# Strassen's identity in half the contraction of a second attention projection, and running product sums kept in one PSUM bank

## The chip, the core and the metric

The kernel runs on one core of one Trainium2 chip. The metric is the device time of one execution in microseconds (us). Three runs of the kernel before gave 2095.98 us in the median, 2095.78 at the least and 2096.19 at the most. PE is TensorE, DVE is VectorE, ACT is ScalarE, POOL is GpSimd and SP is SyncE.

## What is computed

The reference is a stack of layers on a sequence of 256 tokens with 2048 features, all in fp32. A Mamba-2 mixer, a sliding-window attention with a gate, a neighbourhood attention and a squared-ReLU MLP with 8192 hidden features follow each other, each with a residual. The part that the change touches most is the end of the neighbourhood attention and what comes next:

```python
def second_block(x, ...):
    hn = rms_norm(x, norm_mix[layer])
    x = x + neighbourhood_attention(hn, na_w_qkv, ..., na_w_o)   # ends with out @ w_o, 2048 x 2048
    x = x + sq_relu_mlp(rms_norm(x, norm_mlp[layer]), mlp_w1[layer], mlp_w2[layer])
```

`out @ w_o` is a product of 256 x 2048 with 2048 x 2048. The sliding-window attention ends in a product of the same size (`o @ w_out`), and the second half of the MLP (`(a * a) @ w2`) is 256 x 8192 with 8192 x 2048.

## The kernel before, in words

**Units.** All the matrix products are cut into units, 381 of them, listed by `plan` (line 114). A unit is one tile of weights of 128 x 2048 fp32 numbers, 1 MB, that comes from HBM by one DMA (`load`, L997, on SP's queue). Each fp32 number is split into two parts that TensorE multiplies in its fp32r type: ACT copies the tile to `whi` (`high`, L1461), which rounds it, and DVE writes the rest, `wlo = raw - whi` (`low`, L1893). The activations are kept split in the same way, in A1h and A1l or A2h and A2l. A product is then the sum of three: high by high, low by high, high by low.

A unit of form B ("token block") is 512 columns of the result and four 128-row steps of the contraction, for two tiles of 128 tokens: 2 x 4 x 3 = 24 matmuls of 128 x 512 (L1168, L1170, L1172). A unit of form A ("feature block") is 128 columns of the result over the whole contraction. A unit of form P is one product of Strassen's identity in Winograd's form (`product_block`, L1184, L1186, L1188): one token tile only, so 12 matmuls. Seven P units, named a to g in the order a, c, b, d, e, f, g, take the place of four B units: two 512-column blocks ("left" and "right") by two groups of four contraction steps. The other contraction steps of these two blocks stay B units, two for each block.

**What a set of seven needs.** Products b, c, d and f multiply sums of activations. `mixed` (L1921 on DVE, L1838 on ACT, L1924 on DVE) makes them: four additions or subtractions of 128 x 512, four high parts, four low parts. Products b, d, f and g multiply sums of weights. For b and f the second weight tile is added by a DMA from POOL's queue that accumulates into the buffer (`acc`, L2645), and for d and g DVE adds two buffers (`add`, L1904). The results go to the blocks of the residual XR by `drain`: product a is copied by ACT out of its bank to SBUF (`kept`, L1476), d and f are added to that copy by DVE (L1932), and the running sum a, a+d, a+d+f is added to XR (L1860, L1955) from there. A set has 11 such DVE operations and the copy. Eight sets exist: one in the output projection of the sliding-window attention (stage `bo`, products `bp`), and seven in the MLP's second product (stage `down`, products `dp`), where DVE's factor is a column of SM.

**Order of the work.** One list, `script` (line 240), is read by every engine, and each engine takes from it what is its own, in that order, with semaphore waits between. At the step of unit u stand, in this order: the late work on unit u-1 (drain of its last bank), the high split of unit u+2 (it waits until TensorE has done unit u-1, since whi and wlo have three buffers), the low split of unit u+2, sums of weights, the matmuls of u with the drain of its first token tile between, the load of unit u+5, and then what `timetable` (line 174) puts behind unit u. What is put there is written out by hand: attention steps, the activation sums ("mix"), and "x3".

**The stages around the change.** The neighbourhood attention's last group of four heads, step ("na", 3, 0 to 8), ends inside the units of stage `no`: steps 4 to 8 run at units no,0,0 to no,0,2. Stage `no` is sixteen B units: blocks 0 to 3, four contraction groups each. Their results are added to XR (L2086). After block c is complete, the two steps ("x3", c, 0) and ("x3", c, 1) run, one and two units later. The first turns the block with eight transposes on TensorE (`turned`, L1296) and scales, splits and stores it in A1: per chunk, ACT does one scaled copy and one high part twice over (L1688, L1696), DVE two scaled copies and two low parts (L2330, L2339), and each low and high part waits for what the other engine made. The second takes the squares for the RMS norm on ACT (L1706). Chunk c is needed by unit upb,c, the first units of the MLP. The step ("x3", c, 0) stands at unit no,c+1,0 for c = 0, 1, 2, and at upb,0 for c = 3.

Raw tiles go to a ring of three SBUF buffers, of four in some stretches (`wide_ring`, line 454), and the summed weights of a set of seven to one more ("chain", in the work area W). Four PSUM banks serve the units before the MLP in turn. The four others, the side banks, serve attention steps, transposes and the products a, b, d, f of `bp`. In the MLP a planner deals out all eight: each new block takes the bank that has been free longest.

Of the kernel before, what the change touches and what calls it, by code (L numbers as in the profile page):

```python
# [7 lines left out]
P = 128  # L8
# [85 lines left out]
def pair_of(tag):  # L94

    return (1, 2) if tag[0] == "bp" else (2 * tag[2], 2 * tag[2] + 1)


def products(tag):


    top, low = (8, 12) if tag[0] == "bp" else (16 * tag[1] + 8, 16 * tag[1] + 12)
# [11 lines left out]
def plan():  # L114
# [31 lines left out]
    u += in_turn("-a-c-b-d-e-fg--", sevens("bp", "b_w_out", -1, 0),  # L146
# [4 lines left out]
    for nb in range(ND):  # L151
        u += b(("no", nb), "na_w_o_2", nb * 512)
# [21 lines left out]
def timetable(units):  # L174
# [38 lines left out]
    after[at["bo", 2, 0]].append(("mix", -1))  # L213
# [14 lines left out]
    for c in range(ND):  # L228
        run(("x3", c), at["no", c, 3] + 1, 4 if c == ND - 1 else 2)
# [88 lines left out]
def shut(tag):  # L318

    if tag[0] == "down" and seven(tag[1], tag[2]):  # L320
        return (1,) if tag[2] % 2 and tag[3] == 1 else ()
    if tag[0] == "bo" and tag[1] in (1, 2):
        return (1,) if tag[1:] == (2, 1) else ()
    return (0, 1) if tag[0] == "ao" or tag[-1] == 3 else ()


def drains(tag):

    left, right = pair_of(tag)
    return {"a": (), "b": ((1, right, 1), (0, right, 1)), "c": ((0, right, 1),),
            "d": ((0, left, 1), None, (0, right, -1)), "e": ((0, left, 1),), "f": (None, (1, right, -1), (1, left, 1)),
            "g": ((1, left, 1),)}[tag[3]]


def block_of(u, tag, t):
# [5 lines left out]
    return {"c": (s, right, 0), "e": (s, left, 0), "g": (s, left, 1)}.get(name, (u,))  # L343
# [48 lines left out]
def stack_kernel(nc, wst, first, xtok, pos, cols, rows, nabias, consts, out):  # L392
# [7 lines left out]
    with ExitStack() as ctx:  # L400
# [53 lines left out]
        def wide_ring(u):  # L454

            return at["bo", 2, 1] <= u <= at["bo", 3, 3] or u >= at["up", 0, 9]
# [20 lines left out]
        def raw_of(u):  # L477
            if RAW[u] < MLP_ONLY:
                return raw[:, RAW[u], :]
            c = M_RING if RAW[u] == MLP_ONLY else M_CHAIN + 2048 * (RAW[u] - RING)  # L480
# [48 lines left out]
        bp = {x: at["bp", -1, 0, x] for x in "abcdefg"}  # L529
        CLOSES = {(2, 0): (bp["c"], 0), (2, 1): (at["bo", 2, 1], 1), (1, 0): (bp["e"], 0), (1, 1): (bp["g"], 0)}  # L530
        for u, (form, tag, *_) in enumerate(units[:at["up", 0, 4]]):
            if form == "A":
                blocks = [0]
            elif form == "P":
                if tag[3] in "ceg":
                    _, nb, t = block_of(u, tag, 0)
                    BANK[u, 0] = BANK[at["bo", nb, 0], t]
# [7 lines left out]
            for t in blocks:  # L545
                owner = ((u, t) if form == "A" or tag[0] == "ao" else
                         CLOSES.get((tag[1], t), (at.get(tag[:-1] + (3,)), t)) if tag[0] == "bo" else
# [82 lines left out]
        def att_act():  # L630
# [34 lines left out]
        mix_v = Marks(sem("mix_v"), *[words("1 3 2 4 l1 l3 l2 l4")] * (QT + 1))  # L665
        mix_a = Marks(sem("mix_a"), *[words("h1 h3 h2 h4")] * (QT + 1))
# [5 lines left out]
        SIDE, side_before, side_next = {}, [None] * 4, 0  # L672
        EMPTIES = {
# [11 lines left out]
            "bp": lambda x: keep_a(bp["a"]) if x == "a" else evac_v((bp[x], {"b": 1, "d": 1, "f": 0}[x])),  # L685
        }

        def side_uses(s):
# [51 lines left out]
            elif what == "mm" and units[r[0]][1][0] == "bp" and units[r[0]][1][3] in "abdf":  # L740
                yield ("bp", units[r[0]][1][3]), None
# [8 lines left out]
        for x in "abdf":  # L750
            BANK[bp[x], 0] = 4 + SIDE["bp", x][0]
            BEFORE[bp[x], 0] = None, SIDE["bp", x][1]

        def side_free(use):
# [3 lines left out]
        keep_a = Marks(sem("product_kept"), [s[1] for s in SCRIPT if s[0] == "late" and units[s[1]][0] == "P" and  # L758
                                             units[s[1]][1][3] == "a"])


        DRAINS, PIECE, PIECES, EMPTIED = {}, {}, {}, {}
        for s in SCRIPT:
            u = s[1] if len(s) > 1 else None
            if s[0] in ("evac", "late") and units[u][1][0] in ("bo", "bp"):
# [7 lines left out]
        for key, piece in DRAINS.items():  # L773
            u, n = key
            if piece:
                PIECE[key], PIECES[piece[:2]] = PIECES.get(piece[:2]), key
            if not piece or units[u][0] == "B" or None not in drains(units[u][1]):
                EMPTIED[block_of(u, units[u][1], n if units[u][0] == "B" else 0)] = key
        for x in "abcdefg":
            DRAINS.update({(bp[x], n): piece for n, piece in enumerate(drains(units[bp[x]][1]))})  # L780
        FIRST = ((bp["c"], 0), (bp["d"], 0), (bp["f"], 2))
        LAST = {(bp["d"], 2): (0, 2), (bp["e"], 0): (0, 1), (bp["f"], 1): (1, 2), (bp["g"], 0): (1, 1)}
# [4 lines left out]
        for u, (form, tag, *_) in enumerate(units):  # L787
            if u < at["up", 0, 4]:
                continue
            for t in range(NT if form == "B" else 1):  # L790
                block = block_of(u, tag, t) if form != "A" else (u,)
                if block not in WHERE:
                    i = min(range(8), key=lambda i: pool[i][0])
                    WHERE[block], BEFORE[u, t] = i, pool[i][1:]
                    copied = form == "P" and tag[3] == "a"
                    key = u if copied else (u, 0) if form == "A" else EMPTIED[block]
                    assert pool[i][0] <= u, (u, pool)
                    pool[i] = [u + 1 if copied else key[0] + 1, keep_a if copied else evac_v, key]
# [30 lines left out]
        def mix_of(s):  # L829

            c = W_GS if s < 0 else M_MIX
            return W[:, c:c + 2048]

        def parts_of(s):
# [5 lines left out]
            else:  # L840
                yield "1", A1h[:, 0:4, 0:P], A1l[:, 0:4, 0:P], a[:, 1, :, 1, :]
# [7 lines left out]

        def kept(u):  # L850
            if units[u][1][0] == "bp":
                return W[:, W_KT:W_KT + 512]
            c = M_HB + units[u][1][2] * 512
            return W[:, c:c + 512]
# [90 lines left out]
        def residual_ready(t, c, stage):  # L945
# [9 lines left out]
            if stage == "ln1":  # L955
                ends = {(2, 0): (bp["d"], 2), (2, 1): (bp["f"], 1), (1, 0): (bp["e"], 0), (1, 1): (bp["g"], 0)}
                return evac_v(ends[c, t] if c in (1, 2) else (at["bo", c, 3], t))
            if stage == "no":
                return aff_v(("a", t, c), 1)
            return evac_v((at["no", c, 3], t))  # L960
# [1819 lines left out]
```

## Time and profile before

| | |
|---|---|
| median of the three runs | 2095.98 us |
| the profiled execution, its own time | 2096.38 us |
| its span in the profile | 2094.6 us |
| outside the span (launch and end) | 1.8 us |
| TensorE busy in the span | 2088.4 us, 10850 matmuls |
| VectorE busy | 1560.2 us (74%) |
| ScalarE busy | 1144.0 us (55%) |
| DMA | 411.82 MB, 197 GB/s in the mean |

The page gives for every group of instructions the busy time and the mean time of one in ns. A matmul's record overlaps the next one's, so what it costs is the distance between starts and not its own length. In a timeline each row is the start in us from the start of the span, the length in us, the engine, the line of the kernel, and in brackets the idle time of the engine before it with what ended it. `x3` behind a row means three instructions merged.

### The profile page before, as it was taken

The numbers are of one execution on the slowest core, as the hardware profiler recorded it, in microseconds if no ns is written. First come the engines' busy times: TensorE is split into PE (matmuls) and PEld (weight loads), VectorE is DVE, ScalarE is ACT, GpSimd is POOL, SyncE is SP. The second block draws the span as 40 slices with busy tenths as digits, with TensorE's granted clock in tenths as the row PEclk, the third lists the DMA queues.
The fourth block names the chain that finished last, engine by engine and source line by source line (L and its number), as shares of the span: only waits on it lengthen the run. The fifth ranks groups of instructions, "written<-read, shape, count | busy, mean of one in ns | idle before, by whom it ended". The sixth has DMA issues, their size and how long they took to land.

```text
span 2094.6 us, 27475 instructions
## 1 busy us (share of the span) xinstructions
PE 2088.4 (100%) x10850; PEld 1765.6 (84%) x10850; DVE 1560.2 (74%) x2067; ACT 1144.0 (55%) x1425; POOL 53.6 (3%) x44
## 2 busy tenths in 40 slices
PE   9999999999999999999999999999999999999999
PEld 8888888888887888888788888888888888888887
DVE  7798787777778867768875566556778688688775
ACT  6777565565564555665555445454545445444452
POOL 0000000000000000000010011000000000000000
PEclk9999999999999999999999999999999999999999
DMA  8565555564554744447564554455576666566663
GB/s 324 194 239 191 195 210 191 200 211 178 205 192 150 247 160 146 157 151 231 191 211 171 189 181 171 164 181 203 200 221 212 209 221 199 219 188 198 241 181 141
DMA packets 67425, 411.82 MB, mean 197 GB/s; under 512 B 7392, under 2 KB 14304, under 8 KB 19808
## 3 DMA queue, kind: packets, MB, share of 16 engines
q1 hardware_dynamic: 64992, 393.28, 52.3%
q0 software_dynamic: 2304, 16.78, 4.4%
q8 instruction: 86, 1.41, 0.3%
q14 instruction: 43, 0.35, 0.0%
HBM read 407.80 MB, written 2.23 MB: 196 GB/s over the span
## 4 chain that ended last, share of the span: by engine, by line
PE 99%; DVE 1%; ACT 0%; issue 0%; POOL 0%
PE bank L1146 27%; PE bank L1168 15%; PE bank L1170 15%; PE bank L1172 15%; PE bank L1151 14%; PE bank L1188 2%; PE bank L1184 2%; PE bank L1186 2%; PE bank L1266 1%; PE bank L1401 1%; PE bank L1337 1%; PE bank L1359 0%; PE bank L1389 0%; PE bank L1268 0%; PE bank L1296 0%; PE bank L1245 0%
## 5 line engine op out<-in xcount | busy, mean ns | idle before, releaser
L1893 DVE TENSOR_TENSOR wlo<-raw,whi 128x2048 fp32r<-128x2048 f32 x314 | 718.5, 2289 | 217.6 <-ACT whi L1461 186.9
L1461 ACT ACTIVATE whi<-raw 128x2048 fp32r<-128x2048 f32 x314 | 600.2, 1912 | 250.9 <-PE bank L1172 230.7
L1146 PE MATMUL bank<-A,whi 128*128 128x512 f32 x2448 | 587.7, 392 | 0.0
L1146 PEld LDWEIGHTS bank<-A,whi 128*128 128x128 f32 x2448 | 451.1, 188 | 91.8 <-issue 2.4
L1151 PEld LDWEIGHTS bank<-A,wlo 128*128 128x128 f32 x2432 | 311.8, 191 | 11.8
L1151 PE MATMUL bank<-A,wlo 128*128 128x256 f32 x2432 | 315.3, 283 | 0.0
L1168 PE MATMUL bank<-whi,A2h 128*128 128x512 f32 x768 | 301.2, 392 | 0.0
L1170 PE MATMUL bank<-whi,A2l 128*128 128x512 f32 x768 | 299.3, 390 | 0.0
L1172 PE MATMUL bank<-wlo,A2h 128*128 128x512 f32 x768 | 299.1, 389 | 0.0
L1168 PE MATMUL bank<-whi,A 128*128 128x512 f32 x608 | 241.7, 398 | 0.0
L1170 PE MATMUL bank<-whi,A 128*128 128x512 f32 x608 | 237.2, 390 | 0.1
L1172 PE MATMUL bank<-wlo,A 128*128 128x512 f32 x608 | 237.3, 390 | 0.0
L1893 DVE TENSOR_TENSOR wlo<-W,whi 128x2048 fp32r<-128x2048 f32 x63 | 144.2, 2291 | 52.8 <-ACT whi L1461 52.1
L1168 PEld LDWEIGHTS bank<-whi,A2h 128*128 128x128 f32 x768 | 144.2, 188 | 31.0 <-issue 1.4
L1172 PEld LDWEIGHTS bank<-wlo,A2h 128*128 128x128 f32 x768 | 144.2, 188 | 30.4
L1170 PEld LDWEIGHTS bank<-whi,A2l 128*128 128x128 f32 x768 | 144.2, 188 | 29.5
L1461 ACT ACTIVATE whi<-W 128x2048 fp32r<-128x2048 f32 x63 | 120.2, 1914 | 86.5 <-DVE W L1904 55.4
L1168 PEld LDWEIGHTS bank<-whi,A 128*128 128x128 f32 x608 | 114.3, 188 | 24.6 <-issue 2.1
L1172 PEld LDWEIGHTS bank<-wlo,A 128*128 128x128 f32 x608 | 114.1, 188 | 24.6 <-DVE wlo L1873 0.6
L1170 PEld LDWEIGHTS bank<-whi,A 128*128 128x128 f32 x608 | 114.4, 188 | 24.1 <-DVE A L2319 1.0
L1498 ACT ACTIVATE W<-bank 128x256 f32<-128x256 f32 x60 | 23.1, 384 | 179.8 <-PE bank L1151 179.8
L1860 DVE SCALAR_TENSOR_TENSOR XR<-bank,SM,XR 128x512 f32<-128x512 f32 x110 | 80.7, 746 | 18.7 <-PE bank L1172 16.8
(267 smaller groups left out, 1897.6 us busy)
## 6 DMA issues: line engine op xcount, KB each, us to landing
raw<-wst SPq DMA_DIRECT2D x308, 1024.0 KB, 4.8
W<-wst SPq DMA_DIRECT2D x37, 1024.0 KB, 4.9
W<-wst POOLq DMA_DIRECT2D x10, 1024.0 KB, 8.3
W<-cum_scratch SPq DMA_DIRECT2D x8, 1024.0 KB, 7.0
raw<-wst POOLq DMA_DIRECT2D x6, 1024.0 KB, 8.0
W<-rows SPq DMA_DIRECT2D x21, 256.0 KB, 5.9
W<-first SPq DMA_DIRECT2D x12, 384.0 KB, 7.6
W<-exp_scratch SPq DMA_DIRECT2D x16, 256.0 KB, 6.4
```

The lines of the kernel that those rows point to most:

```text
L1146: last = e.matmul(o[:, :], whi[:, s, k * P:(k + 1) * P], A1[:, k, :, :].rearrange("p h t -> p (h t)"), start=k == 0, stop=packed and k == ...
L1151: last = e.matmul(o[:, T:2 * T], wlo[:, s, k * P:(k + 1) * P], A1h[:, k, :], start=False, stop=k == KT - 1)
L1168: e.matmul(o, h, wh, start=opens and k == 0, stop=False)
L1170: e.matmul(o, low, wh, start=False, stop=False)
L1172: last = e.matmul(o, h, wl, start=False, stop=t in shut(tag) and k == 3)
L1184: e.matmul(o, h, wh, start=name in ("a", "b", "d", "f") and k == 0, stop=False)
L1186: e.matmul(o, low, wh, start=False, stop=False)
L1188: last = e.matmul(o, h, wl, start=False, stop=k == 3)
L1461: e.activation(whi[:, u % 3, :], raw_of(u), ACT.Copy).then_inc(*hi.inc((u, 3)))
L1498: e.activation(W[:, M_R + i % 4 * T:M_R + (i % 4 + 1) * T], rest, ACT.Copy).then_inc(*rest_a.inc(u))
L1860: return e.scalar_tensor_tensor(out=o, in0=a, scalar=s, in1=b, op0=op0, op1=op1)
L1893: e.tensor_tensor(wlo[:, u % 3, :], raw_of(u), whi[:, u % 3, :], ALU.subtract).then_inc(*lo.inc((u, 3)))
```

## The change

The neighbourhood attention's output projection gets a set of seven: in blocks 1 and 2, for contraction steps 8 to 15, the four B units become seven P units of a new kind `np` (left is block 2, right is block 1). Stage `no` becomes no,0,0 to no,0,3, then no,1,0; a; no,1,1; c; no,2,0; b; no,2,1; d; no,3,0; e; no,3,1; f; g; no,3,2; no,3,3. Its mix has an addition more, since the heads' outputs are only there as high and low part: DVE first adds A2h and A2l in two operations of 128 x 1024. The mix stands behind no,1,0, before ("x3", 0, 0), which stays there. Steps ("x3", 1, ...) and ("x3", 2, ...) move back to no,3,2, no,3,3 and upb,0. Second, in all the sets the running sum stays in one PSUM bank: d and f accumulate onto a, DVE drains the bank after each of the three, and the copy on ACT and DVE's two additions to it are gone. The core of the diff:

```diff
     u += b(("bo", 0), "b_w_out", 0)
-    u += in_turn("-a-c-b-d-e-fg--", sevens("bp", "b_w_out", -1, 0),
+    u += in_turn("-a-c-b-d-e-fg--", sevens("bp", "b_w_out", -2, 0),
...
-    for nb in range(ND):
-        u += b(("no", nb), "na_w_o_2", nb * 512)
+    u += b(("no", 0), "na_w_o_2", 0)
+    u += in_turn("-a-c-b-d-e-fg--", sevens("np", "na_w_o_2", -1, 0),
+                 [("B", ("no", nb, i), "na_w_o_2", 4 * i, nb * 512) for nb in (1, 2, 3) for i in range(4 if nb == 3 else 2)])
...
-    after[at["bo", 2, 0]].append(("mix", -1))
+    after[at["bo", 2, 0]].append(("mix", -2))
+    after[at["no", 1, 0]].append(("mix", -1))
...
-    for c in range(ND):
-        run(("x3", c), at["no", c, 3] + 1, 4 if c == ND - 1 else 2)
+    run(("x3", 0), at["no", 0, 3] + 1, 2)
+    after[at["no", 3, 2]].append(("x3", 1, 0))
+    after[at["no", 3, 3]] += [("x3", 1, 1), ("x3", 2, 0)]
+    after[at["upb", 0]].append(("x3", 2, 1))
+    run(("x3", 3), at["no", 3, 3] + 1, 4)
...
-    return {"a": (), "b": ((1, right, 1), (0, right, 1)), "c": ((0, right, 1),),
-            "d": ((0, left, 1), None, (0, right, -1)), "e": ((0, left, 1),), "f": (None, (1, right, -1), (1, left, 1)),
-            "g": ((1, left, 1),)}[tag[3]]
+    return {"a": ((0, left, 1),), "b": ((1, right, 1), (0, right, 1)), "c": ((0, right, 1),), "d": ((0, right, -1),),
+            "e": ((0, left, 1),), "f": ((1, right, -1), (1, left, 1)), "g": ((1, left, 1),)}[tag[3]]
...
         def wide_ring(u):
-            return at["bo", 2, 1] <= u <= at["bo", 3, 3] or u >= at["up", 0, 9]
+            return (at["bo", 2, 1] <= u <= at["bo", 3, 3] or at["no", 1, 1] <= u <= at["no", 3, 3] or
+                    u >= at["up", 0, 9])
...
+        for kind, p in (("bp", bp), ("np", np_)):
+            for x in "ab":
+                BANK[p[x], 0] = 4 + SIDE[kind, x][0]
+                BEFORE[p[x], 0] = None, SIDE[kind, x][1]
+            for x, before in (("d", "a"), ("f", "d")):
+                BANK[p[x], 0] = BANK[p["a"], 0]
+                BEFORE[p[x], 0] = evac_v, (p[before], 0)
...
             def load(u):
...
+                    elif RAW[u] >= MLP_ONLY and stage_of(u) == 1 and (before is None or not stage_of(before)):
+                        w.wait_ge(*na_p("v3", 3))
...
             def product_block(u, o):
-                    e.matmul(o, h, wh, start=name in ("a", "b", "d", "f") and k == 0, stop=False)
+                    e.matmul(o, h, wh, start=name in ("a", "b") and k == 0, stop=False,
+                             skip_group_check=name in ("d", "f"))
...
             def late(u):
-                if form == "P" and tag[3] == "a":
-                    w.wait_ge(*mm_done(u))
...
-                    e.activation(kept(u), bank[BANK[u, 0]][:, :], ACT.Copy).then_inc(*keep_a.inc(u))
...
             def mixed(s):
+                elif s == -1:
+                    w.wait_ge(*na_a("h3", 3))
+                    w.wait_ge(*na_v("l3", 3))
+                    for q in range(2):
+                        k = slice(8 + 4 * q, 12 + 4 * q)
+                        e.tensor_tensor(mix_of(s)[:, q * 1024:(q + 1) * 1024].rearrange("p (k t) -> p k t", k=4),
+                                        A2h[:, k, :], A2l[:, k, :], ALU.add).then_inc(*mix_v.inc(f"x{q}", s + 2))
+                    w.wait_ge(*mix_v("x1", s + 2))
...
             def drain(u, n):
-                if not DRAINS[u, n]:
-                    w.wait_ge(*(evac_v((u, 0)) if tag[3] == "d" else evac_v((product(u, "d"), 2))))
-                    e.tensor_tensor(kept(u), ps, kept(u), ALU.add).then_inc(*evac_v.inc((u, n)))
-                    return
```

In the work area, the raw buffer of the fourth ring place in stage `no` is W from N_KT on, and the chain buffer lies over NS and PT. Both are read by the attention's last step until its value products are done (`na_p("v3", 3)`), and so SP waits for these before the load of a.

## Rows read from the trace of the kernel before

**Rows 1.** The page, parts 1, 2 and 4.

```profile
PE 2088.4 (100%) x10850; PEld 1765.6 (84%) x10850; DVE 1560.2 (74%) x2067; ACT 1144.0 (55%) x1425; POOL 53.6 (3%) x44
...
PEclk9999999999999999999999999999999999999999
...
PE 99%; DVE 1%; ACT 0%; issue 0%; POOL 0%
```

**Rows 2.** Stretches: busy us of PE, PEld, DVE, ACT, POOL; clock; DMA share; GB/s.

```profile
949.84:952.56 2.72, 2.72 (x13) 2.25 (x12) 2.62 (x5) 2.08 (x4) 0.00 (x0) 1.00 1.04 220
958.00:960.80 2.80, 2.80 (x14) 2.26 (x12) 2.61 (x3) 1.92 (x1) 0.00 (x0) 1.00 0.21 23
1340.89:1362.75 21.86, 21.86 (x99) 18.06 (x98) 12.57 (x10) 10.99 (x12) 0.00 (x0) 1.00 0.50 190
1492.98:1555.89 62.91, 62.91 (x278) 51.83 (x277) 52.77 (x40) 31.91 (x22) 1.76 (x3) 1.00 0.67 212
```

**Rows 3.** Timeline of TensorE: last attention products, transposes of chunk 0, a wait in bo.

```profile
1324.73 1.89 PE L1401 MATMUL bank<-W 128*128 128x256 f32 x8
...
1340.10 1.03 PE L1296 MATMUL bank<-KO,XR 128*128 128x128 f32 x8
...
1008.26 0.63 PE L1278 MATMUL bank<-KO,XR 128*128 128x128 f32 x4 [0.59 <-DVE XR L2283]
```

**Rows 4.** Timeline of VectorE, stage bo, from unit bo,2,0 to product c.

```profile
946.68 2.29 DVE L1893 TENSOR_TENSOR wlo<-W,whi 128x2048 fp32r<-128x2048 f32 x1 [0.92 <-ACT whi L1461]
...
949.49 2.86 DVE L1921 TENSOR_TENSOR W<-W 128x512 f32<-128x512 f32 x4
952.26 0.69 DVE L1924 TENSOR_TENSOR A<-W,A 128x512 fp32r<-128x512 f32 x1
952.87 1.89 DVE L1924 TENSOR_TENSOR mixr<-W,mixr 128x512 fp32r<-128x512 f32 x3
954.92 4.58 DVE L1893 TENSOR_TENSOR wlo<-raw,whi 128x2048 fp32r<-128x2048 f32 x2 [0.16 <-issue]
```

**Rows 5.** Timeline of ScalarE in the same stretch.

```profile
950.20 0.63 ACT L1838 ACTIVATE A<-W 128x512 fp32r<-128x512 f32 x1 [3.62 <-DVE W L1921]
950.93 2.09 ACT L1838 ACTIVATE mixr<-W 128x512 fp32r<-128x512 f32 x3
952.92 1.91 ACT L1461 ACTIVATE whi<-raw 128x2048 fp32r<-128x2048 f32 x1
```

**Rows 6.** Timeline of VectorE, stage no, from unit no,1,0 on.

```profile
1336.93 2.29 DVE L1893 TENSOR_TENSOR wlo<-raw,whi 128x2048 fp32r<-128x2048 f32 x1 [1.39 <-ACT whi L1461]
1340.74 0.88 DVE L2330 TENSOR_SCALAR W<-bank,CO 128x256 f32<-128x256 f32 x2 [1.51 <-PE bank L1296]
1342.47 0.69 DVE L2339 TENSOR_TENSOR A<-W,A 128x512 fp32r<-128x512 f32 x1 [0.86 <-ACT A L1696]
1343.56 0.69 DVE L2339 TENSOR_TENSOR A<-W,A 128x512 fp32r<-128x512 f32 x1 [0.40 <-ACT A L1696]
```

**Rows 7.** Timeline of ScalarE in the same stretch.

```profile
1334.91 1.92 ACT L1461 ACTIVATE whi<-raw 128x2048 fp32r<-128x2048 f32 x1 [3.52 <-PE bank L1172]
1341.17 0.48 ACT L1688 ACTIVATE W<-bank,CO 128x256 f32<-128x256 f32 x1 [4.34 <-PE bank L1296]
1341.74 0.63 ACT L1696 ACTIVATE A<-W 128x512 fp32r<-128x512 f32 x1
...
1343.36 1.90 ACT L1461 ACTIVATE whi<-raw 128x2048 fp32r<-128x2048 f32 x1
1345.17 0.61 ACT L1706 ACTIVATE W<-XR 128x512 f32<-128x512 f32 x1
...
1346.69 1.92 ACT L1461 ACTIVATE whi<-raw 128x2048 fp32r<-128x2048 f32 x1
```

**Rows 8.** Stage bo: SP issues product a and the tile behind it; the first lands.

```profile
934.70 0.81 SPq L997 DMA_DIRECT2D W<-wst  x2
...
939.55 1.92 ACT L1461 ACTIVATE whi<-W 128x2048 fp32r<-128x2048 f32 x1 [3.38 <-DMA W<-wst]
```

More of the change, by code:

```diff
@@ L342, in block_of @@
     left, right = pair_of(tag)
-    return {"c": (s, right, 0), "e": (s, left, 0), "g": (s, left, 1)}.get(name, (u,))
+    return {"c": (s, right, 0), "e": (s, left, 0), "g": (s, left, 1), "b": (u,)}.get(name, ("sum", s, p))
 def pieces12(x, n):
@@ L739, in side_uses @@
                 yield ("upb", r[0]), r[0]
-            elif what == "mm" and units[r[0]][1][0] == "bp" and units[r[0]][1][3] in "abdf":
-                yield ("bp", units[r[0]][1][3]), None
+            elif what == "mm" and units[r[0]][1][0] in ("bp", "np") and units[r[0]][1][3] in "ab":
+                kind, *_, name = units[r[0]][1]
+                yield (kind, name), None if kind == "bp" else 2 + (name in "bf")
         for s in SCRIPT:
@@ L764, in stack_kernel @@
             u = s[1] if len(s) > 1 else None
-            if s[0] in ("evac", "late") and units[u][1][0] in ("bo", "bp"):
+            if s[0] in ("evac", "late") and units[u][1][0] in ("bo", "bp", "np"):
                 continue
@@ L774, in stack_kernel @@
             u, n = key
[L775 to L782, printed above, removed]
+            PIECE[key], PIECES[piece[:2]] = PIECES.get(piece[:2]), key
+            EMPTIED[block_of(u, units[u][1], n if units[u][0] == "B" else 0)] = key
+        for p in (bp, np_):
+            for x in "abcdefg":
+                DRAINS.update({(p[x], n): piece for n, piece in enumerate(drains(units[p[x]][1]))})
+        LAST = ((bp["d"], 0), (bp["e"], 0), (bp["f"], 0), (bp["g"], 0))
         pool = [[holds[i][0] + 1, evac_v if units[holds[i][0]][1][0] not in ON_ACT else evac_a, holds[i]]
@@ L794, in stack_kernel @@
                     WHERE[block], BEFORE[u, t] = i, pool[i][1:]
[L795 to L796 removed]
+                    key = (u, 0) if form == "A" else EMPTIED[block]
                     assert pool[i][0] <= u, (u, pool)
[L798 removed]
+                    pool[i] = [key[0] + 1, evac_v, key]
+                elif form == "P" and tag[3] in "df":
+                    BEFORE[u, t] = evac_v, (product(u, "a" if tag[3] == "d" else "d"), 0)
                 BANK[u, t] = WHERE[block]
@@ L848, in stack_kernel @@
         xu = W[:, W_XU:W_XU + T]
[L850 to L854, printed above, removed]
         def hidden(i):
@@ L1084, in store @@
             def store(u, n):
-                if DRAINS.get((u, n)) and units[u][1][0] != "bp":
+                if DRAINS.get((u, n)) and units[u][1][0] not in ("bp", "np"):
                     t, nb, _ = DRAINS[u, n]
@@ L1205, in factor @@
                 which = {"b": "1", "c": "4", "d": "2", "f": "3"}[name]
-                return h, low, (mix_a("h" + which, s + 1), mix_v("l" + which, s + 1))
+                return h, low, (mix_a("h" + which, s + 2), mix_v("l" + which, s + 2))
             def dt(n):
@@ L1836, in mixed @@
                 for name, high, _, x in parts_of(s):
-                    w.wait_ge(*mix_v(name, s + 1))
-                    e.activation(high, x, ACT.Copy).then_inc(*mix_a.inc("h" + name, s + 1))
+                    w.wait_ge(*mix_v(name, s + 2))
+                    e.activation(high, x, ACT.Copy).then_inc(*mix_a.inc("h" + name, s + 2))
             def upb(t, n):
```

93 lines of the change are left out of this document (47 added, 46 removed).

## The prediction

> **What bounds the kernel now.** The page comes first: TensorE is busy in all but 6 us of the 2094.6 us span, it is 99% of the chain that ended last, and its clock stands at the upper level in every slice [rows 1]. So only two things can move the time: what TensorE has to do, and how long it stands without work. The stretches come next, since they give what a unit costs. Four B units in a row (96 matmuls) take 21.86 us, 5.46 each. A P unit on A2 takes 2.72 us, one that reads the mixed sums 2.80. In stage `down`, through a whole set of seven, TensorE is busy 62.91 of 62.91 us while DVE is busy 52.77 [rows 2]. DVE is therefore the engine with the least room beside TensorE wherever P units run. The timelines of DVE and ACT in stages `bo` and `no` then show how near the splits are to being late. They are what decides here.
>
> **TensorE's work.** Removed are four B units of stage `no`: 21.86 us. Added are seven P units: a, b, e, g at 2.72, c, d, f at 2.80, in all 10.88 + 8.40 = 19.28 us [rows 2]. The eight transposes of a chunk, 0.79 us between the starts of the first and of the next unit (1340.10 to 1340.89 [rows 2, 3]), are as many as before. Saved: 2.58 us, or 0.12%. With every cover kept that is the whole gain.
>
> **The running sums in one bank.** Per set DVE does 9 drains instead of 11 operations, at about 0.69 us each (as all its 128 x 512 work [rows 4]), and ACT one copy less. That frees about 1.4 us of DVE per set, seven times in the MLP. I cost it at nothing, because TensorE does not wait in the set of seven that the stretch shows [rows 2]; the work that ends last there is TensorE's own. The new waits (d until a is drained, f until d is) are three to four units long, 8 us and more against a drain of 0.69. The sum's bank is held from a to f, but of eight banks I count at most six in use at that point. In `bo` the new drain of a stands between the low splits of c and of bo,1,0: it moves the second from 957.2-959.5 to 957.9-960.1, and bo,1,0 starts at 960.80 (c ends there [rows 2, 4]). Hidden.
>
> **What the mix and x3 do to product c.** This term decides. In `bo`, DVE starts the mix at 949.49, its four operations take 2.86, ACT's four high parts end in time for the high split of c at 952.92, and DVE's low parts end in time for its low split at 954.92, done at 957.2. TensorE starts c at 958.00 [rows 2, 4, 5]. The spare time is 0.8 us, and 1.3 up to the third matmul, the first to need wlo.
>
> In `no` I put the same on the clock of the trace. Unit no,1,0 runs 1334.64 to 1340.10, the transposes to 1340.89 [rows 3], a to 1343.61, no,1,1 to 1349.07, and there c wants whi, and at 1349.5 wlo.
> - DVE is free for the mix at 1336.93 + 2.29 = 1339.2, after the low split of no,1,1 [rows 6].
> - New: two additions of 128 x 1024. The trace has 0.69 us for 512 columns and 2.29 for 2048 [rows 4], so about 1.2 each (bounds 0.69 and 2.29; in between by their columns): 1341.6.
> - Four mixes as in `bo`, 2.86: 1344.5. ACT's high parts end 952.92 - 949.49 = 3.4 us after the mixes' start: 1345.0. DVE's low parts end 5.3 after it: 1346.9 [rows 4, 5].
> - Then, before the high split of c in the common order, comes ("x3", 0, 0). DVE's scaled copies can start only at 1346.9 instead of 1340.74. ACT's first copy is done by then; its first high part starts when DVE's first copy is done, 0.5 later, at 1347.4. From that high part to the next high split it is 1343.36 - 1341.74 = 1.6 us: 1349.0 [rows 6, 7].
> - High split of c, 1.9: 1350.9. Low split, 2.29: 1353.2.
>
> So c's first matmul waits 1.9 us, and its third until 1353.2 instead of 1349.5: TensorE loses 3.7 us. It ends c at 1355.5. Behind the high split, ACT has the squares of chunk 0 (1345.17 to 1346.69, 1.5 us [rows 7]) and then the high split of no,2,0: 1352.4 to 1354.3; its low split ends 1356.7, wanted at 1356.0: 0.7 more. In all 4.4 us. Who waits: only TensorE; DVE's and ACT's later work is paced by it.
>
> After that DVE catches up: going on in the same way, the low splits of b, no,2,1 and d come 1.2 us or more before they are wanted, the addition of weights for d (128 x 2048, so about 2.29) included. The rest that a set adds (three high and three low splits more, two weight additions, nine drains for four) runs in `down` beside TensorE without a wait and leaves DVE 10 of 62.91 us [rows 2]; I cost it at nothing. Without that cover each low split would cost its 2.29.
>
> **The loads.** SP stops at the load of a until the attention's last value products are done, about 1326.6 [rows 3], with the loads of no,1,1, c and no,2,0 queued behind. In `bo` two tiles were issued together from 934.70 and the first was there at 939.55 [rows 8], 4.85 us. So a is there at about 1331.5, its splits (1.92 and 2.29) end at 1335.7, the two additions of block 0 to XR (0.69 each) at 1337.1, and the low split of no,1,1 starts 0.2 later than its 1336.93 before [rows 6]. I take 0 to 0.2, inside the rounding of the term above. POOL's accumulating load for b is issued when a is split, 25 us before b starts.
>
> **The end of the stage.** Three chunks of x3 now run in consecutive units. One needs on ACT 2.2 us (1341.17 to 1343.36), squares 1.5, a high split 1.9, together 5.6 against 6.25 us of TensorE (5.46 + 0.79) [rows 3, 7]. On DVE it is about 4.6 with its waits and a low split 2.29, 6.9, which slips by 0.6 per unit, against some 5 us of lead. The transposes of chunk 3 want the last drain of no,3,3 some 0.2 us after it is done. I take 0, bounds 0 and 1.
>
> **Sum.** -2.58 + 3.7 + 0.7 + 0 = +1.8 us. The profiled execution took 2096.38 us, which gives 2098.2; it stands 0.4 above the median of 2095.98, which gives 2097.8. A measurement of this kernel can tell about 0.2%, 4.2 us, from no change: faster means under 2091.8, slower over 2100.2. The lost time lies between 0 (the chain comes in time) and about 6 (handoffs between ACT and DVE as wide as the 0.40 and 0.86 us seen before low parts [rows 6], the additions at their upper bound).
>
> **Rivals.**
> 1. *The cover holds.* ACT gets c's high split in before 1347, as in `bo`. For it speaks that the same pattern ran in `bo` without a wait; against it that there no x3 step and no additions stood before c. Only the gain is left: 2096.0 - 2.6 = 2093.4.
> 2. *The clock falls at c* (the slower side). TensorE's longest wait in stages `bo` and `no` is 0.59 us [rows 3] and no slice is under the upper level of 2.4 GHz [rows 1], so the trace says nothing of what a stand of 3.7 us, broken by two matmuls, does. If the clock fell to 1.2 GHz behind it, the matmuls of c, no,2,0 and b (11 us) or a part of them would take twice as long: 2 to 8 us more, 2100 to 2106, with 2103 in the middle. It decides only if c starves as forecast. The Trainium skill has such a rule ("TensorE: Matmul & The Clock Gate", Why this matters for your kernels): a long enough gap between bursts of matmuls sends the clock back to half. By that rule the sum would be this rival's; no row here has such a gap.
> 3. *The loads come together* (slower too). If the four queued tiles shared the bandwidth evenly (4.2 MB at the 220 GB/s of rows 2: 19 us), a would land at 1345.6 and not at 1331.5. Up to 1.5 us of lateness hides; the mix would start some 13 us late, and TensorE would lose that: about 2111. Against it stand the 4.85 us of the first of two [rows 8].
> 4. *The sums in one bank are worth time after all*, in a stretch of the MLP where TensorE waits unseen: up to 5 us faster, 2091. TensorE's 6 us outside its busy time over the whole span [rows 1] speak against it. If, the other way, d or f waited for a drain, each of the seven sets would show it.
>
> **Chances.** Starved at c, clock kept: 0.67, alone 2095.2 to 2100.0. Rival 1: 0.19. Rival 2: 0.08. Rival 3: 0.04. Rival 4: 0.02. Faster by over 0.2% comes from rival 4 alone: 0.02. Slower by over 0.2% from rivals 2 and 3 and the upper edge of the first case: 0.15. Within 0.2%: 0.83. The range for 8 in 10 takes in rival 1 and the first case: 2093.2 to 2100.2.
>
> **What the changed profile would show.** 10838 matmuls, bar lost records. In stage `no` a wait of TensorE for whi at c's first matmul of about 1.9 us, then one for wlo of about 1.8, then 0.7 in no,2,0, and none after. On DVE the two 128 x 1024 additions of about 1.2 us directly before four mixes, and x3's copies behind the last low part. On ACT the high split of c behind x3's second high part. Stage `down` at the same 62.9 us. The forecast is wrong if c starts without a wait, if TensorE waits at a or at upb, or if the granted clock leaves the upper level in that stage.

## The result, and the profile after

The changed kernel takes 2099.39 us (median of 22 runs, 2097.25 to 2101.22), the kernel before 2096.16 in as many (2095.57 to 2097.97): a ratio of 1.0014, 95% interval 1.0008 to 1.002. That is 3.2 us more, 1.6 above the forecast, inside its range and within 0.2%. The profiled execution took 2099.29 us, 2.9 more than that of before.

The page of the changed kernel, parts 1 and 4, beside [rows 1]:

```profile
PE 2087.7 (100%) x10838; PEld 1764.6 (84%) x10838; DVE 1567.9 (75%) x2072; ACT 1148.2 (55%) x1424; POOL 55.4 (3%) x46
...
PE 95%; DVE 2%; ACT 1%; DMA 1%; SPq 0%; issue 0%; POOL 0%; DVEq 0%; ACTq 0%
```

TensorE has 12 matmuls less and is busy only 0.7 us less, where 2.6 were to go; and TensorE's share of the chain that ended last has fallen from 99 to 95%. The waits of TensorE there, 1320 to 1420 us (line and what it waited for: us in total, times, longest):

```profile
PE bank L1202 <- DVE wlo L1900: 1.7, 1, 1.7
PE bank L1197 <- ACT whi L1475: 1.5, 1, 1.5
```

Both belong to product c. TensorE's timeline around it:

```profile
1348.96 0.39 PE L1185 MATMUL bank<-wlo,A2h 128*128 128x512 f32 x1
1350.86 0.50 PE L1197 MATMUL bank<-whi,mixr 128*128 128x512 f32 x1 [1.51 <-ACT whi L1475]
1351.19 0.39 PE L1200 MATMUL bank<-whi,mixr 128*128 128x512 f32 x1
1353.24 0.50 PE L1202 MATMUL bank<-wlo,mixr 128*128 128x512 f32 x1 [1.66 <-DVE wlo L1900]
...
1354.33 0.63 PE L1197 MATMUL bank<-whi,mixr 128*128 128x512 f32 x1
1354.76 0.63 PE L1200 MATMUL bank<-whi,mixr 128*128 128x512 f32 x1
...
1357.32 0.54 PE L1183 MATMUL bank<-whi,A2l 128*128 128x512 f32 x1
1357.69 0.39 PE L1185 MATMUL bank<-wlo,A2h 128*128 128x512 f32 x1
```

The two waits stand where they were forecast, and the third matmul starts at 1353.24 for 1353.2. The third wait of the forecast, 0.7 us in no,2,0, is not there. New is what follows from 1354.33 on: the matmuls start 0.43 us apart instead of 0.23. The stretch of its own (columns as in [rows 2]) says why:

```profile
1354.20:1357.60 3.40, 3.40 (x10) 2.65 (x9) 3.40 (x3) 2.04 (x2) 0.00 (x0) 0.50 0.21 27
```

The granted clock is at half, 1.2 GHz, for 3.4 us; just before it and behind it the clock is at 2.4 (1.00 from 1354.00 to 1354.10, 0.94 from 1357.60 to 1357.70). The stretch is too short to show in the page's 40 slices. Here the Trainium skill ("TensorE: Matmul & The Clock Gate", Why this matters for your kernels) has the rule that a long enough gap between bursts of matmuls sends the clock back to half; the trace agrees in direction, since the clock fell behind two gaps, of 1.5 and 1.7 us, with two matmuls between them.

DVE and ACT, beside [rows 6, 7]:

```profile
1339.19 2.35 DVE L1922 TENSOR_TENSOR W<-A2h,A2l 128x1024 f32<-128x1024 f32 x2
1341.58 2.87 DVE L1936 TENSOR_TENSOR W<-W 128x512 f32<-128x512 f32 x4
...
1344.97 1.89 DVE L1939 TENSOR_TENSOR mixr<-W,mixr 128x512 fp32r<-128x512 f32 x3
1346.77 0.87 DVE L2342 TENSOR_SCALAR W<-bank,CO 128x256 f32<-128x256 f32 x2
...
1350.89 2.29 DVE L1900 TENSOR_TENSOR wlo<-raw,whi 128x2048 fp32r<-128x2048 f32 x1 [1.09 <-ACT whi L1475]
```

```profile
1331.55 1.92 ACT L1475 ACTIVATE whi<-W 128x2048 fp32r<-128x2048 f32 x1 [4.46 <-DMA W<-wst]
...
1345.02 0.46 ACT L1695 ACTIVATE W<-bank,CO 128x256 f32<-128x256 f32 x1
1347.28 0.63 ACT L1703 ACTIVATE A<-W 128x512 fp32r<-128x512 f32 x1 [1.80 <-DVE W L2342]
...
1348.91 1.90 ACT L1475 ACTIVATE whi<-raw 128x2048 fp32r<-128x2048 f32 x1
```

The additions start at 1339.19 (forecast 1339.2), the mixes at 1341.58 (1341.6), DVE's low parts end at 1346.8 (1346.9), c's high split starts at 1348.91 (1349.0) and its low split at 1350.89 (1350.9). Before it, ACT stands 1.80 us for DVE's scaled copy of x3: that is the late step that holds c up. The load of a is there at 1331.55 (1331.5).

To compare kernels without what varies elsewhere, I measure stage `no` from the last value products of the attention to the transposes of chunk 3: 1324.73 to 1408.07 before, 83.34 us; 1324.78 to 1410.94 after, 86.16. These 2.8 us are the whole difference between the two profiled executions, within 0.1 us. TensorE's timeline of the changed kernel at these two places:

```profile
1324.78 1.89 PE L1415 MATMUL bank<-W 128*128 128x256 f32 x8
...
1410.94 1.03 PE L1310 MATMUL bank<-KO,XR 128*128 128x128 f32 x8
```

### The profile page after: what moved, and what is told of

Same layout as the page of the kernel before. It is cut to its first block, busy times and chain, and to the rows that moved or that the text cites. A ratio compares the mean times of both kernels' runs of the same rounds, so it can differ in the third digit from the quotient of the medians.

```text
span 2097.5 us, 27442 instructions
## 1 busy us (share of the span) xinstructions
PE 2087.7 (100%) x10838; PEld 1764.6 (84%) x10838; DVE 1567.9 (75%) x2072; ACT 1148.2 (55%) x1424; POOL 55.4 (3%) x46
## 4 chain that ended last, share of the span: by engine, by line
PE 95%; DVE 2%; ACT 1%; DMA 1%; SPq 0%; issue 0%; POOL 0%; DVEq 0%; ACTq 0%
PE bank L1159 26%; PE bank L1181 14%; PE bank L1183 14%; PE bank L1185 14%; PE bank L1164 13%; PE bank L1202 3%; PE bank L1197 3%; PE bank L1200 3%; DVE wlo L1900 1%; PE bank L1280 1%; PE bank L1415 1%; DMA raw<-wst 1%; PE bank L1351 1%; PE bank L1373 0%; PE bank L1403 0%
## 5 line engine op out<-in xcount | busy, mean ns | idle before, releaser
L1900 DVE TENSOR_TENSOR wlo<-raw,whi 128x2048 fp32r<-128x2048 f32 x310 | 709.2, 2288 | 206.5 <-ACT whi L1475 175.8
L1475 ACT ACTIVATE whi<-raw 128x2048 fp32r<-128x2048 f32 x310 | 592.2, 1912 | 229.9 <-PE bank L1185 207.0
L1181 PE MATMUL bank<-whi,A2h 128*128 128x512 f32 x736 | 288.8, 392 | 0.0
L1183 PE MATMUL bank<-whi,A2l 128*128 128x512 f32 x736 | 287.0, 390 | 0.0
L1185 PE MATMUL bank<-wlo,A2h 128*128 128x512 f32 x736 | 286.6, 389 | 0.0
L1900 DVE TENSOR_TENSOR wlo<-W,whi 128x2048 fp32r<-128x2048 f32 x70 | 160.1, 2290 | 62.9 <-ACT whi L1475 62.7
L1475 ACT ACTIVATE whi<-W 128x2048 fp32r<-128x2048 f32 x70 | 133.4, 1914 | 105.7 <-DVE W L1911 66.5
L1181 PEld LDWEIGHTS bank<-whi,A2h 128*128 128x128 f32 x736 | 138.4, 188 | 29.9 <-issue 1.4
L1185 PEld LDWEIGHTS bank<-wlo,A2h 128*128 128x128 f32 x736 | 138.3, 188 | 29.1
L1867 DVE SCALAR_TENSOR_TENSOR XR<-bank,SM,XR 128x512 f32<-128x512 f32 x138 | 100.9, 745 | 18.9 <-PE bank L1185 16.8
```

The source lines that it names most:

```text
L1181: e.matmul(o, h, wh, start=opens and k == 0, stop=False)
L1183: e.matmul(o, low, wh, start=False, stop=False)
L1185: last = e.matmul(o, h, wl, start=False, stop=t in shut(tag) and k == 3)
L1475: e.activation(whi[:, u % 3, :], raw_of(u), ACT.Copy).then_inc(*hi.inc((u, 3)))
L1867: return e.scalar_tensor_tensor(out=o, in0=a, scalar=s, in1=b, op0=op0, op1=op1)
L1900: e.tensor_tensor(wlo[:, u % 3, :], raw_of(u), whi[:, u % 3, :], ALU.subtract).then_inc(*lo.inc((u, 3)))
```

## Experiments

The theory (T): DVE comes too late for c since it has two additions and four mixes to do behind the low split of no,1,1; TensorE stands, and since it stands its clock falls. The rivals are these. R1: the drop of the clock is free or was there anyway, and the stand alone is the loss. R2: the running sums in one bank cost time as well. R3: the additional splits of the set cost time in the stage wherever its pre-work is put. The last column of this table splits the stage at c's third matmul, the first that needs wlo.

| kernel | median us (range, n) | ratio to before, 95% | mean clock | stage, us | to c's 3rd + from it |
|---|---|---|---|---|---|
| changed | 2099.39 (2097.25 to 2101.22, 22) | 1.0014, 1.0008 to 1.002 | 1.0 in 4, 0.999 in 13, 0.998 in 5 | 86.16 | 28.46 + 57.70 |
| changed, again | 2100.01 (2098.06 to 2100.97, 11) | 1.0016, 1.0007 to 1.0025 | 1.0 in 1, 0.999 in 6, 0.998 in 4 | 86.10 | 28.46 + 57.64 |
| x3 later | 2095.09 (2094.22 to 2095.82, 11) | 0.9992, 0.9983 to 1.0001 | 1.0 | 81.95 | other order |
| sums only | 2096.10 (2095.74 to 2097.79, 11) | 0.9998, 0.9989 to 1.0006 | 1.0 | 83.34 | no product c |
| fill | 2097.69 (2097.29 to 2099.24, 11) | 1.0006, 0.9997 to 1.0015 | 1.0 | 85.30 | 28.64 + 56.66 |
| mix early | 2093.54 (2092.68 to 2094.99, 11) | 0.9985, 0.9976 to 0.9994 | 1.0 | 80.94 | 24.88 + 56.06 |
| mix early, again | 2093.73 (2093.48 to 2094.92, 11) | 0.9987, 0.9978 to 0.9996 | 1.0 | 80.94 | 24.88 + 56.06 |
| additions twice | 2101.84 (2100.49 to 2103.19, 11) | 1.0026, 1.0017 to 1.0035 | 0.998 in all | 88.77 | 30.85 + 57.92 |
| twice and fill | 2100.62 (2099.85 to 2101.92, 11) | 1.0021, 1.0012 to 1.003 | 1.0 | 87.53 | 30.91 + 56.62 |
| x3 first | 2101.35 (2100.56 to 2102.55, 8) | 1.0025, 1.0015 to 1.0035 | 0.998 in all | 88.51 | 29.60 + 58.91 |

The kernel before took 2096.67 us beside the first four experiments (33 runs), 2096.27 beside the next four (29) and 2096.39 beside the last (15), which ran on another chip. Its stage `no` is 83.34 us long. In x3 later the transposes of chunk 0 stand behind c, so its two parts can't be set beside the others'. The length of the stage comes from one profiled execution of each kernel.

**x3 later.** The two steps of x3 for chunk 0 stand behind product d and the unit after it, and no longer behind no,1,0 and a:

```diff
-    run(("x3", 0), at["no", 0, 3] + 1, 2)
+    run(("x3", 0), at["np", -1, 0, "d"], 2)
```

> The steps of x3 for chunk 0 stand behind product d and unit no,3,0 instead of behind no,1,0 and a. Theory (c starves because x3's copies and high parts stand, in ACT's order, between the mix and the high split of c): ACT splits c from about 1345.1, DVE from 1346.9 to 1349.1; c starts 0.8 us earlier without the transposes before it, at 1348.3, and waits for wlo 0.3 to 0.5 us. The granted clock stays at its upper level. Span 2094.6 - 2.6 + 0.4 = 2092.4, time 2093.8 (2093.4 to 2094.5), ratio 0.9989. Rival A (the two additions and the mix starve c by themselves): a wait of 2 us or more stays at c, time 2096 or more. Rival B (the time was lost in the sets of the MLP, by waits for the one bank): no wait at c either way, time stays near 2099.

Measured 2095.09, and one wait left:

```profile
1349.66 0.50 PE L1202 MATMUL bank<-wlo,mixr 128*128 128x512 f32 x1 [0.43 <-DVE wlo L1900]
```

ACT no longer stands before the high split of c, so its first matmul does not wait. The low split is still late, since its engine had the additions and mixes to do: 0.6 us lost against the usual distance of 0.23. The stage is 1.4 us shorter than before and 4.2 shorter than with the change as made. So most of the loss, the clock's part included, hangs on x3's place between the mix and c's high split, and a part of the gain comes forth when it goes. The median is 0.6 us above the upper end of what was expected, and its interval still touches 1; the 1.6 us to the median of before agree with the stage's 1.4.

**Sums only.** Stage `no` as before, with four B units per block; of the change only the running sums in one bank stay:

```diff
-    u += b(("no", 0), "na_w_o_2", 0)
-    u += in_turn("-a-c-b-d-e-fg--", sevens("np", "na_w_o_2", -1, 0),
-                 ...
+    for nb in range(ND):
+        u += b(("no", nb), "na_w_o_2", nb * 512)
```

> The second half of the change alone: stage no has its sixteen plain units as before, the running sums stay in one PSUM bank in the eight other sets. Theory (no cover of TensorE is touched): 2096.0, within 0.4 us of before, TensorE busy 62.9 of 62.9 us in the set of stage down, DVE 1.4 us less busy per set. Rival B (d or f wait for the drain of the bank): 0.5 us or more for each of eight sets, 2100 or more. Rival C (less work on DVE and ACT is worth time): 2095 or less.

Measured 2096.10, no change, with the stage at 83.34 as before. A set of seven in `down`, beside the last of [rows 2]:

```profile
1491.38:1554.29 62.91, 62.91 (x285) 52.17 (x284) 51.31 (x40) 31.57 (x22) 1.79 (x2) 1.00 0.64 204
```

DVE is busy 1.46 us less, TensorE exactly as long as before. R2 falls, and so does the prediction's rival 4. One little thing the bank does give: in product g of `bo` the kernel before has its matmuls at 993.88, 994.23 and 994.57, the changed one at 994.17, 994.40 and 994.64. Two distances of 0.35 and 0.34 are 0.23 and 0.24 now, 0.2 us in all. Sums only has them at 995.54, 995.77 and 996.00, so it is the bank's doing.

**Fill.** The change as made, and before c seven matmuls whose result nobody reads, on a free side bank, once b's earlier owner is out of it. TensorE works through most of the time in which it would stand:

```diff
+FILLERS = 7
...
                 s, p, name = units[u][1][1:]
+                if s == -1 and name == "c":
+                    w.wait_ge(*side_free(("np", "b")))
+                    for _ in range(FILLERS):
+                        e.matmul(side[3][:, 0:T], KO[:, 0:P], KO[:, 0:T], start=True, stop=True)
```

> The changed kernel with seven idle matmuls (128 x 256, fp32, into the free bank of product b, about 0.44 us each, 3.1 in all) in front of product c, where TensorE would stand. They add no work that anything waits for. Theory (the clock falls because TensorE stands at c, and this is the difference between the changed kernel's runs): granted clock 1.000 in all runs, c still ends at about 1355.6, stage no,2,0 then waits 0.4 to 0.7 us for wlo, time 2097.3 (2097.0 to 2097.8), which is 1.5 to 2.1 under the changed kernel. Rival (the clock's fall costs nothing, since TensorE would wait for the next split anyway, and the spread has another cause): 2099 to 2099.8. If the fillers themselves delay c: over 2099.4.

The filling and what is left of the waits, in TensorE's timeline:

```profile
1350.05 3.18 PE L1196 MATMUL bank<-KO 128*128 128x256 f32 x14
1352.89 0.59 PE L1202 MATMUL bank<-whi,mixr 128*128 128x512 f32 x1
1353.31 0.40 PE L1205 MATMUL bank<-whi,mixr 128*128 128x512 f32 x1
1354.27 0.50 PE L1207 MATMUL bank<-wlo,mixr 128*128 128x512 f32 x1 [0.56 <-DVE wlo L1905]
1354.60 0.39 PE L1202 MATMUL bank<-whi,mixr 128*128 128x512 f32 x1
...
1357.51 0.50 PE L1186 MATMUL bank<-wlo,A2h 128*128 128x512 f32 x1 [0.18 <-DVE wlo L1905]
```

(The seven float32 matmuls show as 14.) The clock stays up in all 11 runs. c's third matmul comes about as late as in the changed kernel, 28.64 us after the stage's start for 28.46, and yet from there to the stage's end it takes 56.66 us instead of 57.70. So the slow clock costs a net 1.0 us in the profile, and R1 falls. That is less than the slow matmuls seem to cost (eight distances from 1354.33 to 1357.69 are 3.36 us, at 0.23 they would be 1.84): with the clock up, the wait in no,2,0 is there, as forecast, at 1357.51; with the clock down TensorE comes later to that matmul and finds wlo ready. By the medians fill is 1.7 us under the changed kernel and 2.3 under its repetition, which ran beside other experiments. Its profiled execution, 2099.24, is the slowest of the eleven, with a wait of 1.3 us ahead of 104 us, outside the stage; so the stage is compared here and not the two profiled times.

**Mix early.** The mix stands behind no,0,2 instead of no,1,0, in the time in which DVE and ACT have little to do while the load of a is under way:

```diff
-    after[at["no", 1, 0]].append(("mix", -1))
...
+    after[at["no", 0, 2]].append(("mix", -1))
```

> The mix of the new set stands behind unit no,0,2, where DVE was idle for 6 us, instead of behind no,1,0; x3 stays where the change has it. Theory: additions and mixes end at about 1333, ACT splits a at 1333.3 to 1335.2 and DVE to 1337.5, no,1,1 to 1341.1, x3 of chunk 0 ends at 1344, c is split by 1348 and wanted at 1349.5: no wait over 0.3 us in stage no, clock at its upper level, time 2096.0 - 2.6 = 2093.4 (2093.1 to 2094.0), ratio 0.9988. Rival A (the load of a, held back until the last value products, makes a or no,1,1 late once something else stands there): a wait of 1 us or more at a or no,1,1, time 2094.5 to 2097.

Measured 2093.54 and, in a repetition, 2093.73. TensorE doesn't wait once in the stage, and the clock is up:

```profile
1323.00:1420.00 97.00, 97.00 (x444) 80.48 (x443) 75.87 (x67) 56.06 (x62) 2.89 (x4) 1.00 0.63 215
```

On DVE the additions now start directly behind the last split of the attention's output, and the mix is done before the low split of a:

```profile
1325.67 0.81 DVE L2583 TENSOR_TENSOR A2l<-bank,A2h 128x256 fp32r<-128x256 f32 x2
1326.52 2.36 DVE L1922 TENSOR_TENSOR W<-A2h,A2l 128x1024 f32<-128x1024 f32 x2
1328.91 2.87 DVE L1936 TENSOR_TENSOR W<-W 128x512 f32<-128x512 f32 x4
...
1332.31 1.89 DVE L1939 TENSOR_TENSOR mixr<-W,mixr 128x512 fp32r<-128x512 f32 x3
1334.35 2.29 DVE L1900 TENSOR_TENSOR wlo<-W,whi 128x2048 fp32r<-128x2048 f32 x1 [0.15 <-issue]
```

The low split of a starts 1.9 us later against the stage's start than in the changed kernel (10.64 for 8.77), and nobody waits for it. The stage takes 80.94 us, 2.40 less than before, in both. With the 0.2 us in `bo` that makes 2.6, beside 3.1 and 2.7 by the medians. R3 falls: TensorE waits for nothing that the set adds once its mix is out of the way. This version is faster than both kernels; its two intervals against before stay under 1.

**Changed, again.** The changed kernel once more, beside the next three.

> The changed kernel once more, beside the next three on the same chip. Theory: a granted clock under 1.000 in most of its runs and about 2099.4 there, 2097.3 to 2098 in the runs where the clock stays; the profile shows a lower clock only at product c and just behind it.

Measured 2100.01. The waits are 1.50 and 1.65 us, and the mean clock is under 1.000 in 10 of 11 runs. In this profile the clock falls before c's third matmul, and not 1 us behind its start as in the first:

```profile
1351.60:1353.40 1.80, 0.23 (x1) 0.00 (x0) 1.80 (x2) 1.71 (x4) 0.00 (x0) 1.00 0.00 0
1353.40:1356.80 3.40, 3.32 (x8) 2.65 (x9) 3.05 (x4) 2.67 (x2) 0.00 (x0) 0.50 0.00 0
```

The third matmul starts at 1353.48. The low stretch is again 3.4 us long and the stage 86.10 us. What the runs at 0.998 look like no profile shows.

**Additions twice.** The two additions are made a second time, which puts DVE 2.35 us further behind:

```diff
-                    for q in range(2):
-                        ...
-                    w.wait_ge(*mix_v("x1", s + 2))
+                    for r in range(2):
+                        for q in range(2):
+                            ...
+                        w.wait_ge(*mix_v(f"{'yx'[r]}1", s + 2))
```

> The two additions of 128 x 1024 in front of the mix are made twice (same result), 2.35 us more of DVE work before c's splits. Theory (every us of that chain is a us of TensorE at c): the waits at c for whi and wlo grow from 3.5 to about 5.9 us, all of it in the first; without a fall of the clock 2097.4 + 2.35 = 2099.8, and with the clock's fall, in nearly all runs, 1 to 2.5 us more, median 2101 to 2102.3, clock 0.998 or 0.999. Rival (DVE has room there, the wait at c is set by ACT or by the loads): less than 1 us over the changed kernel.

The timeline of TensorE and the stretch around c:

```profile
1353.04 0.80 PE L1197 MATMUL bank<-whi,mixr 128*128 128x512 f32 x1 [3.89 <-ACT whi L1475]
1353.63 0.63 PE L1200 MATMUL bank<-whi,mixr 128*128 128x512 f32 x1
1355.42 0.80 PE L1202 MATMUL bank<-wlo,mixr 128*128 128x512 f32 x1 [1.16 <-DVE wlo L1900]
```

```profile
1349.00:1352.50 3.50, 0.14 (x1) 0.00 (x0) 2.21 (x5) 2.94 (x4) 0.00 (x0) 1.00 0.00 0
1352.60:1359.30 6.70, 5.11 (x11) 3.61 (x12) 5.88 (x5) 5.32 (x7) 0.00 (x0) 0.50 0.00 0
1359.50:1362.00 2.50, 2.50 (x13) 2.06 (x12) 2.50 (x3) 1.92 (x1) 0.00 (x0) 1.00 0.97 298
```

DVE's 2.35 us come back whole: c's third matmul comes 30.85 us after the stage's start for 28.46, and the stage is 2.7 us longer than that of the changed kernel beside it. Nothing between DVE and TensorE had room there. The mean clock is 0.998 in every run; in the profile it is low for 6.7 us, and it falls while TensorE stands, not at its next matmul. The time lies in the range expected.

**Twice and fill.** The same, with twelve idle matmuls before c.

> The kernel with the additions made twice, and twelve idle matmuls (5.2 us) in front of c. Theory: clock 1.000 in all runs, 2099.8 (2099.4 to 2100.6): the difference to the same kernel without the idle matmuls, 1 to 2.5 us, is the clock's. Rival (a stand of TensorE costs nothing beyond itself): the same time as without them, or more.

The clock is up in all 11 runs, and the median is at the upper end of what was expected (2100.6). c's third matmul comes at the same time (30.91), but the way from there to the end takes 56.62 us for 57.92. The slow clock costs 1.3 us by the profiles and 1.2 by the medians. The clock's fall, and not the length of the wait, makes this part: the filler changes only what TensorE does while it would stand.

**x3 first.** x3's step for chunk 0 stands before the mix, behind the same unit:

```diff
-    after[at["no", 1, 0]].append(("mix", -1))
...
     run(("x3", 0), at["no", 0, 3] + 1, 2)
+    after[at["no", 1, 0]].append(("mix", -1))
```

> Behind unit no,1,0 the step of x3 stands before the mix, not behind it. Theory (the order model of the prediction: both stand between no,1,0 and the high split of c, so the order alone gives nothing back): x3 ends at 1344.2 on DVE, additions 1346.6, mixes 1349.5, ACT's high parts 1350.0, high split of c 1350.0 to 1351.9, low split to 1354.2; waits at c 4.7 us instead of 3.5, time 1 us over the changed kernel, median 2100 to 2101, fewest 2098.4. Rival (x3's delayed copies alone are the trouble): the stand shrinks to 1 us or less, 2094.5.

Measured 2101.35: 1.3 us over the changed kernel beside it, where the theory had 1 us, and a little over the range (2100 to 2101). The waits at c are 2.6 and 1.7 us, 4.3 in all for 4.7. The rival, a stand of 1 us or less, is refuted. DVE's timeline shows where the time goes:

```profile
1340.61 0.88 DVE L2342 TENSOR_SCALAR W<-bank,CO 128x256 f32<-128x256 f32 x2 [1.50 <-PE bank L1310]
1342.34 0.69 DVE L2351 TENSOR_TENSOR A<-W,A 128x512 fp32r<-128x512 f32 x1 [0.86 <-ACT A L1703]
1343.43 0.69 DVE L2351 TENSOR_TENSOR A<-W,A 128x512 fp32r<-128x512 f32 x1 [0.40 <-ACT A L1703]
1344.04 2.36 DVE L1922 TENSOR_TENSOR W<-A2h,A2l 128x1024 f32<-128x1024 f32 x2
```

In this order DVE itself stands, 1.5 us for the transposes and 1.3 for ACT's copies, and the mix begins 4.85 us later than in the changed kernel (1344.04 for 1339.19). c's third matmul comes 1.1 us later (29.60). The clock is low for 6.6 us and more, from before that matmul (1354.20) on:

```profile
1353.50:1360.10 6.60, 5.90 (x14) 4.64 (x15) 6.25 (x5) 4.46 (x3) 0.00 (x0) 0.50 0.16 56
```

Most of it lies on matmuls that run one behind the other. It costs about 2.3 us, an estimate: 58.91 for the 56.6 us that both kernels with idle matmuls take from c's third matmul on. This order has no run of its own with the clock up. Of the two bad orders the change had taken the better one. That the clock is low for longer here than the 3.4 us of the changed kernel was not foreseen.

**Mix early, again.**

> The kernel with the mix behind unit no,0,2 a second time, on whatever chip it comes to. Theory: 2.6 to 3.0 us under before, ratio 0.9986 to 0.9988, its interval clear of 1, clock at its upper level in every run. Rival (the first 3.1 us were partly the start-up wait before 104 us, which differs from run to run): 2 us or less.

The same stage length to 0.01 us, and 2093.73 for 2093.54.

## Why the prediction was right, and where not

**The direction and the mechanism at c held; the clock did not.** By its own signs the forecast was wrong in one point: it named a granted clock that leaves the upper level in stage `no`, and that came. Here are its terms, with the profile's figures from the table:

| term | forecast | measured |
|---|---|---|
| seven P units for four B units | -2.58 | -2.40 (mix early) |
| product c stands | +3.7 | +3.58 (28.46 - 24.88) |
| wait in no,2,0 | +0.7 | +0.60 (56.66 - 56.06, with the clock up) |
| clock | 0 (rival 2) | +1.04 (57.70 - 56.66) |
| end of the stage | 0 | 0 |
| sums in one bank | 0 | 0 in stage `no`, 0.2 us gained in `bo` |
| sum | +1.8 | +2.82 (stage: 2.82) |

**The saving** is 0.18 us less than forecast. In mix early the seven products take 19.40 us from start to start, for 19.28; 0.10 of that is product a (2.82 for 2.72), which stands directly behind the transposes. The rest is in the B units: the eight behind the transposes of chunk 0 take 43.80 us, where eight of before take 43.73 in the mean.

**Product c** came as forecast: up to its low split each start on DVE and ACT was within 0.15 us, and the high split of no,2,0 came 0.26 us early (1352.14 for 1352.4). The wait in no,2,0 is a difference of two kernels; in fill's own timeline it is some 0.45 us (distances of 0.57 and 0.34 where 0.23 is usual), so the forecast 0.7 was somewhat high. That the chain at c came out so closely came from following each engine's list in its order, x3 included, and not from comparing busy shares: DVE is busy for 75% of the span, and yet one place in it decides.

**The step that failed is the clock, which the sum put at nothing**: the chance of rival 2, and with it its price. I gave "starved at c, clock kept" 0.67 and the clock's fall 0.08, on the ground that no row showed a long stand. Given the stand that I had forecast, the mean clock was under 1.000 in 18 of 22 runs, and in 10 of 11 of the repetition. The runs fall into groups by their mean clock: four at 1.000 (middle 2097.36 us), thirteen at 0.999 (2099.29), five at 0.998 (2100.14). Three of the first four (2097.25 to 2097.40) lie 0.4 to 0.6 us under the forecast of 2097.8; the fourth took 2099.53, as long as the next group, and why stays open. So the median lies 1.6 us above the forecast because most runs are in the other two groups. In the profile the stage's terms explain 1.0 of it: 1.04 from the clock, and -0.04 from all the others together. That the median came out inside the range is partly luck: the room above the forecast had been put there for wider handoffs, and the clock used it. The price was put at 2 to 8 us, with the remark that a part of c, no,2,0 and b would run at half. It was 1.0 us by the profiles of runs at 0.999, and 1.3 by those of additions twice and twice and fill; by the medians some 1.9 to 2.8 between these groups, and 1.2 between the two kernels with the additions twice. The groups' medians differ by more than the profiles' stage does, and how much of that is something else stays open: TensorE's wait for line L2171's data ahead of 104 us, which has nothing to do with the change, is 0 to 1.7 us long in the profiles of these kernels. The rule of the Trainium skill that stood beside rival 2 ("TensorE: Matmul & The Clock Gate", Why this matters for your kernels) pointed the right way; the missing row was taken for evidence against it, which it was not.

**Rival 1** (the cover holds, 2093.4) is what the early mix makes of the kernel: 2093.5 and 2093.7. As the change stands it is refuted. **Rival 3** is refuted: the load of a was there at 1331.55, although SP had issued five loads from 1326.69 to 1329.20. Its price was too high as well: at the 404 GB/s that the last row of this document shows, four tiles that share evenly are there after 10 us, at about 1337, and c would have been some 4 us later and not 13 (an estimate from these rows). **Rival 4** is refuted by sums only.

**What hides the rest** held too: the splits of b, d and e, the weight additions and the chunks of x3 at the end of the stage cost nothing. No other wait of TensorE is seen from 1360 to 1420 us in any of the kernels.

## What to carry over

A product that saves work on the bounding engine brings its preparation onto the engine that feeds it, and whether it pays is decided by where that preparation stands in this engine's list: here the stage is 5.2 us longer with these operations behind no,1,0 than behind no,0,2, where TensorE waits for none of them. So put them where the feeding engine stands idle and the inputs are just there. If TensorE is forecast to stand for some microseconds, forecast the clock as well. In the kernels here that stood for 3.1 us or more around two matmuls it fell in 47 of 52 runs, and in the one that stood for 0.4 us in none of 11. Its price is the work that runs at half, less the waits behind it that it swallows. Where the stand can't be removed, idle matmuls that fill it kept the clock in 22 of 22 runs; with them c's third matmul came 0.2 and 0.1 us later (28.64 for 28.46, 30.91 for 30.85).

## What was new of the hardware

- A stand of 1.5 us, two matmuls, and a stand of 1.7 us lowered the mean clock in 28 of 33 runs, not in all; in both profiles the clock was at 1.2 GHz for 3.4 us. The longer stands (3.9 and 1.2; 2.6 and 1.7) did so in all 19 runs, in the profiles for 6.6 to 6.8 us. In three of these four profiles the fall came while TensorE stood, in one 1 us behind the start of the matmul that followed. With idle matmuls in their place the clock was at 1.000 in 22 of 22 runs.
- Loads moved at about twice the kernel's mean rate, whether queued or alone. From 1337 to 1340 us, where loads of the stage are still queued, the stretch of the changed kernel shows 404 GB/s, and the mean of the page is 197. It isn't the queue that makes them fast: the kernel before issues its loads one by one there, and from 1320 to 1345 us its slices with a load under way reach 433 GB/s. Between them its DMA stands.

```profile
1337.00:1340.00 3.00, 3.00 (x15) 2.49 (x14) 3.00 (x3) 0.00 (x0) 0.33 (x1) 1.00 1.02 404
```
